# Hybrid encoder step: where VectorE takes the weight sums of the next feed-forward step

## The reference

```python
def conv_ffn(xn, prev, w_up, conv_w, w_down):
    u = xn @ w_up                                   # 1024 -> 2 x 2816
    uc, new = causal_dwconv(u, prev, conv_w)        # y = up[:, 0:L]*w[0] + up[:, 1:L+1]*w[1] + up[:, 2:L+2]*w[2]
    a, g = jnp.split(uc, 2, axis=-1)
    return (jax.nn.silu(g) * a) @ w_down, new
...
x = x + y_mixer
x = x + conv_ffn(rmsnorm(x, norm2), ...)
y = rmsnorm(x, final_norm)
```

## Time and profile before

| | |
|---|---|
| median of 3 runs | 2705.91 us (2700.77 to 2707.47) |
| profiled execution, its own time | 2706.28 us |
| its span, first to last instruction | 2704.6 us |
| mean granted TensorE clock | 0.943 |
| PE busy | 2415.4 us (89%) |
| PE weight load busy | 2190.8 us (81%) |
| DVE busy | 1806.8 us (67%) |
| POOL busy | 1243.0 us (46%) |
| ACT busy | 1061.1 us (39%) |

### The profile page before, as it was taken

How to read it: one execution, slowest core, us unless ns; L and a number is a source line. 1 busy time by engine, 2 the same in 40 slices (tenths; PEclk the granted TensorE clock), 3 DMA queues, 4 the chain that set the end, 5 groups by cost and what they waited for, 6 DMA issues and landing times.

```text
span 2704.6 us, 38439 instructions
## 1 busy us (share of the span) xinstructions
PE 2415.4 (89%) x13090; PEld 2190.8 (81%) x13090; DVE 1806.8 (67%) x2588; ACT 1061.1 (39%) x2055; POOL 1243.0 (46%) x770
## 2 busy tenths in 40 slices
PE   7999969999699975999999978999999878888896
PEld 6899758998598955888888867888888767777785
DVE  2055640456505565888888887888888977777777
ACT  5233343333433333333333354343443453343333
POOL 3132412224133226556655555566555745555552
PEclk9999979999799997999999988999999988888888
DMA  5121352113522234221122243221222341222221
GB/s 161 34 63 32 139 176 63 47 47 117 179 79 57 99 119 178 71 70 58 58 70 70 90 153 96 70 63 53 70 70 70 109 140 59 70 70 70 70 62 53
DMA packets 244716, 231.41 MB, mean 86 GB/s; under 512 B 8060, under 2 KB 216273, under 8 KB 244625
## 3 DMA queue, kind: packets, MB, share of 16 engines
q1 hardware_dynamic: 244625, 230.18, 27.0%
HBM read 197.32 MB, written 32.83 MB: 85 GB/s over the span
## 4 chain that ended last, share of the span: by engine, by line
PE 52%; DVE 13%; issue 7%; POOL 5%; ACT 5%; DMA 2%; SPq 0%; DVEq 0%; ACTq 0%; POOLq 0%
PE ps L1163 17%; PE ps L1165 16%; PE ps L1164 16%; DVE up_y L1749 6%; POOL hid_lo L759 3%; DVE resid L1732 2%; POOL wq_lo L731 2%; ACT up_y L1037 1%; ACT wq_hi L1007 1%; ACT up_y L1045 1%; DMA x_in<-in_x_prompt_dram 1%; ACT r L1090 1%; DVE xo L1709 1%; DVE y_n L1485 0%; DMA out_dram<-y_n 0%
## 5 line engine op out<-in xcount | busy, mean ns | idle before, releaser
L1163 PE MATMUL ps<-xo,wq_hi 128*128 128x384 f32 (+1 forms) x1848 | 615.3, 333 | 59.7 <-ACT r L1090 24.4
L1165 PE MATMUL ps<-xo,wq_hi 128*128 128x384 f32 (+1 forms) x1848 | 613.8, 332 | 0.0
L1164 PE MATMUL ps<-xo,wq_lo 128*128 128x384 f32 (+1 forms) x1848 | 613.7, 332 | 0.0
L731 POOL TENSOR_TENSOR wq_lo<-wu_sum,wq_hi 128x512 fp32r<-128x512 f32 x264 | 371.3, 1417 | 392.5 <-ACT wq_hi L1007 392.5
L417 POOL TENSOR_TENSOR w_lo<-raw,w_hi 128x1024 fp32r<-128x1024 f32 x96 | 235.1, 2456 | 624.6 <-ACT w_hi L412 624.6
L1732 DVE TENSOR_TENSOR resid<-resid,ps 128x512 f32<-128x512 f32 (+1 forms) x748 | 496.1, 680 | 37.6 <-PE ps L1165 25.6
L1163 PEld LDWEIGHTS ps<-xo,wq_hi 128*128 128x128 f32 x1848 | 364.9, 197 | 82.2 <-issue 55.0
L1749 DVE SCALAR_TENSOR_TENSOR up_y<-up_u,params,up_y 128x768 f32<-128x768 f32 (+1 forms) x264 | 370.2, 1402 | 89.4 <-ACT up_y L1037 64.7
L1163 PE MATMUL ps<-wd_hi,hid_hi 128*128 128x512 f32 x704 | 297.1, 422 | 140.3 <-POOL hid_lo L759 109.0
L1164 PEld LDWEIGHTS ps<-xo,wq_lo 128*128 128x128 f32 x1848 | 365.4, 198 | 21.8
L1165 PEld LDWEIGHTS ps<-xo,wq_hi 128*128 128x128 f32 x1848 | 364.9, 197 | 0.0
(11 more groups left out here) (191 smaller groups left out, 3833.3 us busy)
## 6 DMA issues: line engine op xcount, KB each, us to landing
wu_raw<-in_w_up_dram SPq DMA_DIRECT2D x132, 512.0 KB, 5.1
raw<-in_w_in_dram SPq DMA_DIRECT2D x72, 512.0 KB, 3.9
wd_raw<-in_w_down_dram SPq DMA_DIRECT2D x66, 512.0 KB, 5.8
x_in<-in_x_prompt_dram SPq DMA_DIRECT2D x32, 512.0 KB, 4.4
raw<-in_w_out_dram SPq DMA_DIRECT2D x24, 512.0 KB, 3.4
xo_raw<-x_ops SPq DMA_DIRECT2D x14, 768.0 KB, 7.6
x_mid<-resid SPq DMA_DIRECT2D x16, 512.0 KB, 2.6
resid<-x_mid SPq DMA_DIRECT2D x16, 512.0 KB, 6.0
```

Source lines behind the costliest of these rows:

```text
L731: pool.tensor_tensor(wq_lo[:, i, :], wu_source(i), wq_hi[:, i, :].bitcast(F32), ALU.subtract).then_inc(wu_lo, 1)
L1163: pe.matmul(out, lh, rh, start=(first and n == 0), stop=False, skip_group_check=skip)
L1164: pe.matmul(out, ll, rh, start=False, stop=False, skip_group_check=skip)
L1165: last = pe.matmul(out, lh, rl, start=False, stop=end, skip_group_check=skip)
```

## The change

In VectorE's feed-forward step the call `sum_up(g + 1)` (four operations of 128x512 each, with their waits for the loaded weights and for `wu_lo`) moves from behind `tail(1)` to behind the `put` of c22. All 65 calls inside the steps move; the one ahead of the first step stays.

```diff
                 tail(1)
                 if edge == 0 and b:
                     low_x(b, 5)
-                if more:
-                    sum_up(g + 1)
                 if edge == 1:
                     dve.wait_ge(resid_ready[0], 16 * 4 * (b + 1))
                 head(2)
...
                 dve.wait_ge(up_done, NP * g + 5)
                 dve.wait_ge(r3_read, g + 1)
                 put(b, 1, 2, r_3, c22_read)
+                if more:
+                    sum_up(g + 1)
                 head(4)
                 if edge == NF - 1 and b + 1 < NB:
                     low_x(b + 1, 0)
```

## The result

The changed kernel takes 2924.83 us (median of 4 runs, 2920.9 to 2927.3) against 2704.89 for the kernel before on the same chip: ratio 1.0813, 95% interval 1.0793 to 1.0833, slower by 220 us. The forecast was 3023 us with a range of 2860 to 3085: the direction and the range held, the size was 98 us too large. What the prediction called its forecast's own range, 2940 to 3080, missed by 15 us.

The account below looks back on a forecast made before the run. TensorE alternates with one chain through VectorE, ScalarE and GpSimd. 40 steady steps of blocks 0 and 1 at +6.1 us (244), 19 of block 2 at +3.6 (68) and edges 5 give +317: 3023 us, range 2860 to 3085.

Parts of the forecast that it names:

- forecast's own range: Whole kernel: 2940 to 3080 us, from 40 steps at +5.2 to +6.8, block 2 +2 to +4.5, edges -8 to +15.
- The step that bounds: Steady feed-forward step, c22 to c21: 2.6 us of sums against 1.40 us idle, making c21 and the taps late.
- The turns with GpSimd: VectorE's taps and product alternate whole instructions with GpSimd's remainders; with the lateness, +3.25 us a step.
- three places: Where VectorE waits for GpSimd: first tap behind wd_lo, second pair of taps, product behind the last remainder.
- The taps keep their lengths: Sign of being wrong: tap pairs staying as before (2.98 and 3.00 us), where over 3 us was expected for both.
- The clock: TensorE in blocks 0 and 1: idle grows from 0.95 to 4.2 us, clock halves for 5.9 us, +2.9 us a step.
- Block 2: Its clock loss is already paid; VectorE, ScalarE lateness and GpSimd turns give about +3.6 us in each of 19 steps.
- Edges: Nothing for steps 0 and 1 of blocks 1 and 2; 5 us for the last steps of blocks 0 and 1.
- the clock stays up: Rival: the delay is real but TensorE's clock does not fall in blocks 0 and 1; 2909 us, chance 0.14.
- Only the lateness: Rival: GpSimd turns hardly matter, only ScalarE's lateness counts, about +1.1 us in 59 steps; 2771 us, chance 0.12.

Follow-up runs that it names:

- e3: The changed kernel, but GpSimd makes the seventh weight's remainder behind hid_lo, not in front of it: 2838.66 us, ratio 1.0491.
- e2: The changed kernel, but ScalarE scales the gate half ahead of roundings 2 to 4 of the next weights: 2903.43 us, ratio 1.0734.
- e4: The changed kernel, but TensorE fills idle time with unread products, 12 a step in blocks 0 and 1, 24 in block 2: 2821.66 us, ratio 1.0431.
- e8: The changed kernel with the seventh remainder behind hid_lo and unread TensorE products (6 in blocks 0 and 1, 24 in block 2): 2773.46 us, ratio 1.0272.

## Why the prediction was right, and by how much it missed

- The step that bounds: right. The sums had slack where they stood and less than they need behind c22. In block 0 c21 was late by 0.75 us (0.96 forecast), ScalarE's scaling by 1.15 (1.35), the first tap by 0.98 (1.1).
- The turns with GpSimd: right in kind, mis-sized. I summed +3.25 us a step from c22 to hid_lo; in the block 0 steps shown it was +1.95 (c22 to the next down product 17.63 us before, 19.58 after). Of the three places, the product behind the last remainder cost what I had (+1.0, and e3 takes it away). In block 0 the first tap behind wd_lo cost nothing, since the first sum starts 0.48 us behind c22 and not 0.68, so everything ran 0.2 us sooner and wd_lo was over; e2, with the tap sooner, shows the wait that I had expected (1.40 us). The second pair had one turn, as before, where I had two. In block 1 it was the other way round: the first tap, 0.18 us later, lost its turn (+1.1, to the remainder behind wd_lo), the product didn't. In no block did all the turns that I had summed come together. "The taps keep their lengths" stood among my signs of being wrong, and in block 0 they did, 3.0 us a pair. A walk of this length decides such turns by tenths of a microsecond, and I had none to spare.
- The clock: right that it falls in blocks 0 and 1, mis-sized. I took 2.9 us from block 2; down product to c22 grew by 1.6 us in the mean of block 0 and 1.9 in block 1. Behind the idle time of 3 us, where I had 4.2, the low stretch mostly lasts 3 us, not 5.9; only 7 of 37 steps have one of 6 us. e4 gives the loss back, e3 shows it coming and going. Why the low stretch is mostly half as long as in block 2 no run here settles.
- Together a steady step of blocks 0 and 1 grew by 3.6 and 4.1 us instead of 6.1, the term that was mis-sized: 143 us over 37 steps, where 6.1 gives 226.
- Block 2: +2.3 us a step in the mean, I had +3.6. In the steps shown the way from c22 to the next down products grew by 3.3 (15.45 to 18.73 us), but 1.4 came back before c22 (3.0 and 0.8 in the means). The idle time split by ScalarE's r_1 goes with it, and the low stretch that now falls elsewhere; no run takes the split away, so that this is the cause is argued and not shown. I had looked there for a wait, not for what it does to the clock.
- Edges: +31 us for the ten edge spacings and the first c21. My +5 is not their counterpart, since my sum had four of these steps among its steady ones: with them it gives 3 x 6.1 + 3.6 + 5 = 27 us. That it comes near is luck. That the last step of a block holds ScalarE's rounding of the next activations behind the sums was in the program order, and I priced it at 2.5 us each instead of 7.7.
- The rival "the clock stays up" (2909 us) is nearest in time, but for a wrong reason: the clock did fall, and the turns were cheaper. "Only the lateness" describes what is left in block 0 of e8. The stated range held because it had been stretched down to take in that rival; by the forecast's own range of 2940 to 3080 the time was missed. The mechanism was right in each part, and the hit owes something to that width.

## What to carry to other kernels

Before moving work into an engine's idle time, compare the length of the work with that idle time (2.6 us into 1.40), and then follow the first result that another engine waits for: in-order queues behind it (ScalarE's scaling, the edge's rounding) move with it. An order that puts the remainder nobody needs yet behind the one TensorE waits for gave 2.65% for one moved line, and keeping TensorE busy with unread products gave 1.2% in a stretch where its clock fell each step; together 2615.21 us, 3.1% under the kernel before and 10.6% under the changed one.

## What the runs showed of the hardware

In block 0 of e3 the same 2 us of idle time in front of TensorE's down products was followed by a low clock (1.2 GHz) in 12 of 19 steady steps and not in the other 7 (26.6 against 25.1 us a step). In the kernel before, with 0.7 to 1.1 us, it was in none of the 37 steady steps of blocks 0 and 1; in the changed kernel, with 2.8 to 3.3 us, in all 37. In the rows shown a VectorE operation with two SBUF operands and a GpSimd operation took turns where both were pending: 1.95 us for a product of 0.96, 4.06 for a pair of 3.00, 1.61 for a sum of 0.68. VectorE's adds from PSUM did not: in the feed-forward layer of the changed kernel some 400 of 128x512 ran beside a GpSimd operation for over 0.5 us, and none took more than 0.69.
